# Splitting and multiplying four rows of the first output projection inside the Fourier stage

## The reference

```python
def fourier_mix(u):
    b, n, e = u.shape
    ug = u.reshape(b, n, N_FOURIER_GROUPS, FOURIER_GROUP_DIM).astype(jnp.float32)
    f = jnp.fft.fft2(ug, axes=(1, 3), norm='ortho').real
    return f.reshape(b, n, e).astype(u.dtype)

def gated_out(o, g, w_out):
    return (o * jax.nn.silu(g)) @ w_out

# in each layer, with gt from the conditioning vector
xp = xp + gt_p * op
xs = xs + gt_s * os_
```

## Time and profile before

| | |
|---|---|
| median of the runs | 2153.98 us |
| profiled execution | 2157.06 us |
| its span, first to last instruction | 2155.2 us |
| TensorE busy | 2096.4 us, 97% |
| VectorE busy | 1384.9 us, 64% |
| ScalarE busy | 923.2 us, 43% |
| mean granted TensorE clock | 0.989 |

### The profile page before, as it was taken

One profiled execution on the slowest core, in us unless ns is written; L12 is line 12 of the kernel. 1 busy time (PEld: TensorE's weight loads), 2 busy tenths in 40 slices (PEclk: granted clock), 3 DMA queues, 4 the chain that ended last, 5 costly groups with the idle time before them and its releaser, 6 DMA issues. The chain is left out here.

```text
span 2155.2 us, 33197 instructions
## 1 busy us (share of the span) xinstructions
PE 2096.4 (97%) x13347; PEld 2030.1 (94%) x13347; DVE 1384.9 (64%) x2062; ACT 923.2 (43%) x1738; POOL 1.6 (0%) x8
## 2 busy tenths in 40 slices
PE   6999999989999999999999999999999999999997
PEld 4999977989999999999999999989999999989997
DVE  7887864664258888888754422238888888875223
ACT  7321242242134333333433333337777777764220
POOL 0000000000000000000000000000000000000000
PEclk9999999999999999999999999999999999999998
DMA  8653442694234444555544544361444433307332
GB/s 334 200 181 134 137 154 96 251 321 154 65 119 169 154 145 146 157 160 145 171 162 174 212 159 157 137 231 69 167 167 167 167 147 137 123 1 269 106 129 88
DMA packets 125976, 342.70 MB, mean 159 GB/s; under 512 B 14465, under 2 KB 69889, under 8 KB 116609
## 3 DMA queue, kind: packets, MB, share of 16 engines
q1 hardware_dynamic: 125824, 340.61, 45.8%
HBM read 225.70 MB, written 114.82 MB: 158 GB/s over the span
## 5 line engine op out<-in xcount | busy, mean ns | idle before, releaser
L254 PE MATMUL o_ps<-o_y_hi,o_w 128*128 128x384 f32 x768 | 197.7, 337 | 9.9 <-DVE o_y_lo L2352 9.2
L2783 DVE TENSOR_REDUCE a_nmax<-a_ps 128x1 f32<-128x1152 f32 x127 | 171.8, 1353 | 51.0 <-PE a_ps L2591 51.0
L254 PE MATMUL a_ps<-o_y_hi,o_w 128*128 128x384 f32 x768 | 196.3, 335 | 1.2 <-DVE o_x_early L2360 0.7
L2625 PE MATMUL a_ps<-a_v_hi,a_at_hi 128*128 128x256 f32 x576 | 173.8, 302 | 0.0
L2692 ACT ACTIVATE a_e<-a_ps,a_nmax 128x1152 f32<-128x1152 f32 x127 | 155.4, 1224 | 34.2 <-DVE a_nmax L2783 34.2
L2625 PE MATMUL a_ps<-a_v_lo,a_at_hi 128*128 128x256 f32 x576 | 163.0, 283 | 0.0
L2625 PE MATMUL a_ps<-a_v_hi,a_at_lo 128*128 128x256 f32 x576 | 162.8, 283 | 0.0
L254 PEld LDWEIGHTS o_ps<-o_y_hi,o_w 128*128 128x128 f32 x768 | 140.3, 190 | 10.6 <-DVE o_y_lo L2352 9.3
L254 PEld LDWEIGHTS a_ps<-o_y_hi,o_w 128*128 128x128 f32 x768 | 138.8, 188 | 2.1 <-DVE o_x_early L2360 1.1
L2352 DVE TENSOR_TENSOR o_y_lo<-o_y_raw,o_y_hi 128x384 fp32r<-128x384 f32 x94 | 51.1, 556 | 133.1 <-ACT o_y_hi L2301 133.1
L2701 ACT CAST a_at_hi<-a_ps 128x512 fp32r<-128x512 f32 (+1 forms) x192 | 91.5, 476 | 91.0 <-PE a_ps L2606 91.0
(11 more groups left out here) (370 smaller groups left out, 5781.8 us busy)
## 6 DMA issues: line engine op xcount, KB each, us to landing
p_w_raw<-w_in_dram SPq DMA_DIRECT2D x32, 1024.0 KB, 4.9
o_y_raw<-y_dram SPq DMA_DIRECT2D x96, 192.0 KB, 3.6
g_wada<-w_ada_dram SPq DMA_DIRECT2D x32, 512.0 KB, 4.5
f_w_raw<-w_u_dram SPq DMA_DIRECT2D x32, 512.0 KB, 4.4
o_w_raw<-w_out_dram SPq DMA_DIRECT2D x28, 512.0 KB, 5.0
g_dram<-g_stage SPq DMA_DIRECT2D x16, 576.0 KB, 3.1
f_g<-g_dram SPq DMA_DIRECT2D x8, 1152.0 KB, 7.7
y_dram<-f_y SPq DMA_DIRECT2D x8, 1152.0 KB, 5.5
```

The source lines that it names most:

```text
L254: mm = pe.matmul(ps[:, d, 0:CH], a, m, start=(e == 0 and j == 0), stop=(e == ET - 1 and j == 2))
L2625: mm = pe.matmul(ps[:, out_bank(at_step), 0:UC], a, x, start=(kt == 0 and j == 0), stop=(kt == TT - 1 and j == 2))
L2783: dve.tensor_reduce(nmax[:, m % 2, half:half + 1], ps[:, 3 * half:3 * half + 3, 0:CH], AX.XY, ALU.max, negate=True).then_inc(maxed, 1)
```

## The change

Rows 0 to 3 of w_out and the y tiles 0 to 3 of chunk 0 get a raw tile of their own, `stage`, with 8 KB for each row. SP issues the four loads of w in iteration 2 of the Fourier stage ahead of the wait for `gated`, and the four loads of y between the store of y of unit 2 and the load of g of unit 5. Iteration 6 now loads the second set: w rows 4 to 7 and the y tiles that follow in the order.

ScalarE splits the staged operands behind unit 6's casts (w for output tiles 4 and 5, 512 columns each, and the four y tiles) and behind unit 7's (w for tiles 6, 7 and 3). VectorE makes their low halves ahead of `gate(5)`, `gate(6)` and `gate(7)`. TensorE multiplies rows 0 to 3 for the output tiles 4 to 7 behind spectra(7), within the Fourier block, into the banks 0 to 3, and tiles 3, 0, 1, 2 at the start of the projection's block; PSUM is kept over the boundary, and output tile d of layer 0 has another bank. Then the projection goes on at row 4. `gate(n)` starts at a new semaphore, `halves_done` (the end of L1882), and waits for `chan_done` before the context columns; the `spectrum_lo` between its parts move by one place each. The split y tiles of layer 0 lie in other places, ScalarE waits for the last y stores at row 10, and `ab_lo` has its own address. Layer 1 keeps its order.

```diff
+    STAGED = (4, 0)
+    BANKS = ((5, 6, 7, 4, 0, 1, 2, 3), range(DT))
+    STAGED_D, WAITING_D, LATER_D = (4, 5, 6, 7), 3, (0, 1, 2)
...
+    def staged_raw(self, d):
+
+        return self.stage[:, :, BANK + d * P:BANK + (d + 1) * P]
+
+    def staged_hi(self, act, d, done):
+        act.copy(self.w[:, d, 0, 0:self.staged, :], self.staged_raw(d)).then_inc(done, 1)
+
+    def staged_lo(self, dve, d, done):
+        dve.tensor_tensor(self.w[:, d, 1, 0:self.staged, :], self.staged_raw(d), self.w[:, d, 0, 0:self.staged, :].bitcast(F32),
+                          ALU.subtract).then_inc(done, 1)
...
+    def load_next(self, eng, y_src, w_src):
+        for p, (c, e) in enumerate(self.order[self.NR:2 * self.NR]):
+            self.load_y(eng, y_src, self.NR + p, c, e)
+            self.load_w(eng, w_src, self.staged + p)
...
                 if n == H - 2:
                     sp.wait_ge(tok_done, first_piece[H - 1] + 4)
-                    ahead(sp)
+                    following.load_next(sp, y_rows, w_out)
+                if n == 2:
+                    sp.wait_ge(tok_done, first_piece[3] + 4)
+                    for e in range(following.staged):
+                        following.load_w(sp, w_out, e)
                 sp.wait_ge(gated, n + 1)
                 sp.dma_start(y_d[n], y[:, s]).then_inc(y_out[s], 16)
+                if n == 2:
+                    sp.wait_ge(y_out[1], 16)
+                    for e in range(following.staged):
+                        following.load_y(sp, y_rows, e, 0, e)
                 if n + 3 < H:
                     sp.dma_start(g[:, n % 3], g_d[n + 3]).then_inc(g_in[n % 3], 16)
...
+                mm.then_inc(halves_done, 1)
                 if n >= 1:
                     pe.wait_ge(ctx_gated, n)
...
+            def staged_products(k, es):
+
+                pe.wait_ge(following.ahead_lo, k + 1)
+                for e in es:
+                    pe.wait_ge(following.y_lo_done, e + 1)
+                    following.products(pe, ps, following.STAGED_D[k], e)
+
+            for es in (range(0, 2), range(2, 4)):
+                for k in range(2):
+                    staged_products(k, es)
+            staged_products(2, range(4))
+            pe.wait_ge(gated, H - 1)
+            staged_products(3, range(4))
...
+                if n == H - 2:
+                    for e in range(following.staged):
+                        act.wait_ge(following.w_in[e], 16)
+                    for d in following.STAGED_D[0:2]:
+                        following.staged_hi(act, d, following.ahead_hi)
+                    for e in range(following.staged):
+                        following.first_y_hi(act, e)
+            act.wait_ge(tok_done, first_piece[H - 1] + 4)
+            for d in (*following.STAGED_D[2:4], following.WAITING_D):
+                following.staged_hi(act, d, following.ahead_hi)
...
-                dve.wait_ge(chan_done, n + 1)
+                dve.wait_ge(halves_done, n + 1)
...
-                if n + 2 < H:
-                    spectrum_lo(n + 2, 0)
+                dve.wait_ge(chan_done, n + 1)
...
                 if n + 2 < H:
-                    spectrum_lo(n + 2, 1)
+                    spectrum_lo(n + 2, 0)
...
             for n in range(H):
+                if n == H - 3:
+                    for k in range(2):
+                        staged_lo(k)
+                if n == H - 2:
+                    for e in range(2):
+                        following.first_y_lo(dve, e)
+                if n == H - 1:
+                    for e in range(2, 4):
+                        following.first_y_lo(dve, e)
+                    dve.wait_ge(chan_done, H)
+                    for k in range(2, 5):
+                        staged_lo(k)
                 gate(n)
...
+            if staged:
+                for k, d in enumerate((tiles.WAITING_D, *tiles.LATER_D)):
+                    if k == 0:
+                        pe.wait_ge(tiles.ahead_lo, len(tiles.STAGED_D) + 1)
+                    else:
+                        pe.wait_ge(tiles.later_lo, k)
+                    for e in range(staged):
+                        mm = products(d, e)
+                        if k == len(tiles.LATER_D):
+                            mm.then_inc(e_done, 1)
             for c in range(LAST):
-                for e in range(ET):
+                for e in range(staged if c == 0 else 0, ET):
...
+            if staged:
+                for d in tiles.LATER_D:
+                    tiles.staged_hi(act, d, tiles.later_hi)
+                act.wait_ge(tiles.later_lo, len(tiles.LATER_D))
             for e in range(ET):
+                if staged and e == 6 + staged:
+                    for semaphore, count in stored:
+                        act.wait_ge(semaphore, count)
```

More of the change, by code:

```diff
@@ L218, in tile @@
             return nc.alloc_sbuf_tensor_at(f"o{layer}_{name}", shape, F32, offset=sh.base + offset)
+        self.staged, self.banks = self.STAGED[layer], self.BANKS[layer]
+        if self.staged:
+            self.stage = tile("stage", [P, self.staged, 4 * BANK], 114688)
         self.y_raw = tile("y_raw", [P, self.NR, CH], 180224)
@@ L229, in __init__ @@
         self.x_out = [nc.alloc_semaphore(f"o{layer}_x_out{d}") for d in range(DT)]
+    LAG = 4
+    order = []
+    for e in range(ET):
+        order += [(0, e)] + ([(1, e - LAG)] if e >= LAG else [])
+    for e in range(ET - LAG, ET):
+        order += [(1, e)]
+    for e in range(ET):
+        order += [(2, e)]
     def begin(self, nc, sh, layer):
-        w_at, y_at = ((49152, 0), (0, 131072))[layer]
+        w_at = (49152, 0)[layer]
         def at(name, shape, offset):
@@ L252, in products @@
     def products(self, pe, ps, d, e):
-        for j, (a, m) in enumerate(passes(self.w[:, d, 0, e, :], self.w[:, d, 1, e, :], self.y_hi[:, e, :], self.y_lo[:, e, :])):
-            mm = pe.matmul(ps[:, d, 0:CH], a, m, start=(e == 0 and j == 0), stop=(e == ET - 1 and j == 2))
+        for j, (a, m) in enumerate(passes(self.w[:, d, 0, e, :], self.w[:, d, 1, e, :], self.y[0][e], self.y[1][e])):
+            mm = pe.matmul(ps[:, self.banks[d], 0:CH], a, m, start=(e == 0 and j == 0), stop=(e == ET - 1 and j == 2))
         return mm
     def w_hi(self, act, e, ds=slice(0, DT)):
[L258 to L261, removed]
+        act.wait_ge(*self.row_in(e))
         act.copy(self.w[:, ds, 0, e, :], self.raw(e, ds)).then_inc(self.w_hi_done, 1)
     def w_lo(self, dve, e, ds=slice(0, DT)):
-        dve.wait_ge(self.w_hi_done, e + 1)
+        dve.wait_ge(self.w_hi_done, e - self.staged + 1)
         dve.tensor_tensor(self.w[:, ds, 1, e, :], self.raw(e, ds), self.w[:, ds, 0, e, :].bitcast(F32),
@@ L1603, in _, with fourier_mix @@
                     own_attention(j, at)
[L1606 removed]
+def fourier_mix(nc, sh, fold, w_u, w_ny, g_d, y_d, dft_tok, dft_chan, following, y_rows, w_out):
     with ExitStack() as ctx:
@@ L2133, in out_project @@
         LAST = NCH - 1
-        if layer == 0:
-            tiles.begin(nc, sh, layer)
-        AHEAD = (0, 2)[layer]
-        if AHEAD > 0:
-            for semaphore in (tiles.ahead_hi, tiles.ahead_lo):
+        staged = tiles.staged
+        AHEAD = staged or 2
+        for semaphore in (tiles.ahead_hi, tiles.ahead_lo):
+            sh.own(semaphore)
+        if staged:
+            for semaphore in (tiles.later_hi, tiles.later_lo):
                 sh.own(semaphore)
-        w, y_hi, y_lo = tiles.w, tiles.y_hi, tiles.y_lo
         done_x = at("done_x", [P, LAST, DT, CH], 0)
-        w_raw, y_raw, x, sq, NR = tiles.w_raw, tiles.y_raw, tiles.x, tiles.sq, tiles.NR
-        if ps is None:
-            ps = ctx.enter_context(nc.psum_tensor(f"o{layer}_ps", [P, 8, BANK], F32))
+        x, sq, NR, banks = tiles.x, tiles.sq, tiles.NR, tiles.banks
+        LOADED = 2 * NR if staged else NR
         for semaphore, count in stored:
@@ L2166, in out_project @@
             y_stored = sem("y_stored")
-        LAG = 4
-        order = []
-        for e in range(ET):
-            order += [(0, e)] + ([(1, e - LAG)] if e >= LAG else [])
-        order += [(1, e) for e in range(ET - LAG, ET)] + [(2, e) for e in range(ET)]
-        place = {step: k for k, step in enumerate(order)}
+        LAG = tiles.LAG
+        place = {step: k for k, step in enumerate(tiles.order)}
         def chunk(c):
@@ L2195, in _ @@
             for e in range(ET):
-                if e >= tiles.NW:
-                    sp.wait_ge(w_lo_done, e - 3 if e < tiles.NW + 2 else e - 1)
+                p = e - staged
+                if p >= tiles.NW:
+                    sp.wait_ge(w_lo_done, p - 3 if p < tiles.NW + 2 else p - 1)
                     tiles.load_w(sp, w_src, e)
@@ L2373, in normalise @@
                 dve.scalar_tensor_tensor(tile, tile, sh.final_g[:, d:d + 1], factor, ALU.mult, ALU.mult).then_inc(normed, 1)
+            if staged:
+                for k, d in enumerate(tiles.LATER_D):
+                    dve.wait_ge(tiles.later_hi, k + 1)
```

(1 more changed line is left out.)

80 lines of the change are left out of this document (52 added, 28 removed).

## The result

The changed kernel takes 2143.0 us, median of six executions (2140.9 to 2147.4), against 2153.8 for the kernel before in the same session: ratio 0.995 [0.994, 0.996], 10.8 us less. Five executions on another chip gave 2145.2 against 2154.4, ratio 0.9957 [0.9943, 0.997], 9.2 less. The forecast was 8.6 less.

What follows compares the result with a forecast made beforehand. TensorE, busy 2096.4 of 2155.2 us, was taken as the bound, leaving its idle time and slow clock to win. 11.7 - 0.8 - 2.3 = 8.6 us less gave a median of 2145.4 us, range 2142.9 to 2150.5.

Steps and rivals of the forecast that it cites:

- The hole and its echo: Between Fourier stage and first out projection: TensorE idles 9.2 us, then slow clock costs 2.5; filling it wins 11.7 us.
- The operands: Late Fourier stage: ScalarE's added casts (3.3 us) and VectorE's low halves (5.7 us) fit; VectorE's end covered by 1.3 us.
- The boundary: Barrier ending the Fourier block: still costs TensorE 0.8 us, bounds 0.4 and 3.3, too short to slow the clock.
- The loads: Fourier units: 2.89 MB added to the shared queue delays small row loads, mainly unit 7's; TensorE loses 2.3 us.
- The 2 us behind the last byte: DMA fixed cost that would land unit 7's rows at 441.8 and make the loss 3.8 us; rejected from the trace.
- Behind the boundary: Start of the projection: y row 4 ready with 1.5 us of cover after the last y store, TensorE runs on as before.
- A: Rival: rows do not wait behind the added loads, or the queue has more room; loss 0 to 0.5, 2143.3 us; 15%.
- the prediction's own sign: Fourier units: TensorE waits of some 1 us ahead of unit 5's and unit 7's spectra if right; none would show otherwise.
- B: Rival: queue costs about 3 us more, through unit 7's rows, the last y store or staged y tiles; 2148.4 us; 25%.
- C: Rival: new VectorE order starves the token stage in every unit; 3.4 us slower, 2157.4 us; 4%.
- D: Rival: the hole only moves, within the staged products or after the barrier, with slow clock; gain under 3 us, 2152; 6%.

Runs made afterwards that it cites:

- Experiments 1: Changed kernel with all 48 staged products moved from the Fourier block to the start of the next block, loads and splits kept; 2154.6 us, ratio 1.0.
- 2: Changed kernel with 24 of the 48 staged products (tiles 6 and 7) moved to the start of the projection; 2149.2 us, ratio 0.9979.
- 3: Changed kernel with the gating's old order, waiting for all of a unit's spectra, low halves back where they stood; 2145.2 us, ratio 0.9963.
- 5: Kernel before with only the eight added loads (2.89 MB), into a free buffer read by nobody; 2157.2 us, ratio 1.001.
- 6: Changed kernel with the four staged w rows issued behind the store of y of unit 2, not ahead of it; 2145.6 us, ratio 0.9954.
- 7: Changed kernel with two staged w rows issued ahead of the store of y of unit 2 and two behind; 2144.8 us, ratio 0.9952.
- 9: Changed kernel with 1.05 MB of further unused loads in iteration 2 among the staged w rows; 2148.3 us, ratio 0.9969.
- 10: Changed kernel with 1.76 MB of further unused loads in iteration 2 among and behind the staged w rows; 2150.0 us, ratio 0.9978.
- experiment 4: Kernel before with only the new order of the gating and its low halves; 2153.3 us, ratio 0.9994.
- experiment 11: Kernel before with the load of g issued ahead of the store of y in every unit; 2156.2 us, ratio 1.0004.

## Why the prediction was right, and where its sum was off

**The hole and its echo, 11.7 us: right.** 135.92 - 125.02 = 10.9, with 0.3 at the boundary and 0.3 in the units given back, is 11.5. Experiments 1 and 2 show it by moving the products back.

**The operands: right.** ScalarE and VectorE in the changed kernel's unit 6, and VectorE's last low halves and last step of gating:

```profile
424.10 1.14 ACT L290 CAST o_w<-o_stage 128x512 fp32r<-128x512 f32 x2
...
425.14 1.76 ACT L326 CAST o_y<-o_stage 128x384 fp32r<-128x384 f32 x4
426.19 1.27 DVE L293 TENSOR_TENSOR o_w<-o_stage,o_w 128x512 fp32r<-128x512 f32 x2
...
440.42 1.88 DVE L293 TENSOR_TENSOR o_w<-o_stage,o_w 128x512 fp32r<-128x512 f32 x3
...
446.43 0.67 DVE L2195 TENSOR_TENSOR f_y<-gf_ps,f_g 1x512 f32<-1x512 f32 x1
```

The casts take 2.9 us (3.3 forecast), the low halves 5.2 in all (5.7). VectorE ends at 447.1 and TensorE at 448.4: 1.3 us of cover, as forecast.

**The boundary, 0.8: too dear.** It measured 0.3, less than the 0.4 of the lower bound. The 0.8 came from a boundary at which VectorE was last and ScalarE first; here TensorE is last and first.

**The loads, 2.3 us: the term that failed.** The step was "the queue is full while it moves, 357 GB/s, so 6.6 us a unit". Measured: TensorE lost 0.34 in the units. The changed kernel's queue while the added loads drain, and the microsecond after:

```profile
414.00:433.00 19.00, 18.88 (x159) 18.77 (x158) 16.42 (x48) 7.87 (x19) 0.00 (x0) 1.00 1.03 415
433.00:434.00 1.00, 1.00 (x11) 1.00 (x10) 1.00 (x3) 0.64 (x2) 0.00 (x0) 1.00 0.60 235
```

With work always waiting the queue moves 415 GB/s, not the 357 of the earlier trace rows, which is a mean over bursts that begin on an idle queue. By this rate, from the end of unit 1's transfers at 409.3: 7.08 MB of three units and the new 2.89 take 24.0 us, to 433.3, and it ran empty near 433.6. The last small packets, the rows of unit 7, pass by 434.0, and unit 7's spectra start at 435.58: about 1 us of slack, their landing counted, where the prediction had 2.3 of loss. At unit 5 there is almost none, and there the prediction was nearer: it had 0.9 of loss, and experiments 2, 3, 5, 6, 7 and 9 each show TensorE standing for the rows (0.15 to 1.84 us), until about 0.6 us after their last packet. The 2 us behind the last byte, which the prediction weighed from the Trainium skill (DMA: Bandwidth & Descriptors, section Anatomy of one DMA) and turned down, do not show for these rows; the page gives the figure for transfers that GpSimd issues, and here SP issues them. The row from which the rate could have been taken stood in the trace of before: 413 GB/s at a share of 1.03 behind the hole; its neighbour in the earlier trace rows, with a backlog too, has 384. The prediction took 384 for the new loads alone and the mean with its start for the rest.

**What it did not see: the stores.** A store of y issued behind the added loads lands in 10.5 us:

```profile
y_dram<-f_y SPq DMA_DIRECT2D x1, 1152.0 KB, 10.5
```

against 5.3 before, and VectorE may not write the next gated tile into that buffer until it has. VectorE, and the token product behind it:

```profile
420.01 1.22 DVE L2169 TENSOR_TENSOR f_y<-gf_ps,f_g 128x1024 f32<-128x1024 f32 x1 [2.40 <-DMA y_dram<-f_y]
```

```profile
422.79 0.19 PEld L1917 LDWEIGHTS gf_ps<-f_tok_hi,f_u_hi 128*128 128x128 f32 x1 [0.23 <-DVE f_ab_lo L2152]
```

2.40 us on VectorE come out as 0.2 to 0.3 on TensorE, which is all that the loads cost here. But neither this path nor that of the rows has cover left: experiment 9 turns one more megabyte into 4.1 us, on both. The prediction bounded the loads by the small rows alone and never named the path of the stores; its range held the time without having weighed it.

**Behind the boundary: right.** VectorE waits for the last y store and has y row 4 ready in time:

```profile
454.33 0.56 DVE L2465 TENSOR_TENSOR o_y<-o_y_raw,o_y 128x384 fp32r<-128x384 f32 x1 [0.80 <-DMA y_dram<-f_y]
```

It ends at 454.9; TensorE reaches row 4 at 448.67 + 8.3 = 457.0, 2.1 us later (1.5 forecast).

**The rivals.** A has the nearest time, 2143.3, in part for its reason (more room in the queue), and by the prediction's own sign, no waits ahead of the spectra of units 5 and 7, it is A that came; its other reason, that rows do not queue, is refuted by experiment 6. B was a real neighbour: experiments 9 and 10 are B, by the rows of unit 5 and a store of y where it named unit 7's rows and the last store. C is refuted by experiment 4, though the wait it describes, the fourth token piece for the low half of the first, is the one by which a late store reaches TensorE. D did not occur.

**The order of the gating: a gain of 1.1 us** (experiment 3) that the prediction used for VectorE's idle time and did not price by itself. It is why the boundary is 0.3 and not 0.7 and why less is lost in the units.

## What to carry to other kernels

Work that needs nothing from the stage's end belongs in front of the barrier, where TensorE would otherwise pause: it pays the pause and the slow clock behind it, here a fifth of the gain. Before loads are put in front of others in a queue, follow all that queues behind them, stores above all, to the engine that may not overwrite their source; and size the queue by its rate with a backlog, not by the mean over bursts. Ask how many microseconds are left before the queue, not the engine, decides: here none ahead of a store or of the small rows, and one more megabyte, 2.5 us of transfer, cost 4.1. And where a profile names a releaser, check in the code that the instruction waits for that one and when it ended: in experiment 9 it had not been waited for at all.

## What was not expected of the hardware

- One queue moved 415 GB/s over 19 us with a backlog and 357 over a burst from idle. Within such bursts some 2 us run at 217 to 295 GB/s, read from windows of 1 us. With store and load exchanged (experiment 11) the slow part stays; its cause is open.
- A pause of 3.70 us was followed by 3.4 us at granted clock 0.51, the 8.21 us of experiment 1 by some 5. In experiment 9 two pauses of 1.2 and 1.3 us with 1 us of work between were followed by 3.2 us at 0.50; behind the single wait of 1.84 in experiment 6 it stayed at 1.00.
- Where TensorE waited for the small row loads (2.3 KB), it started some 0.6 us after their last packet: their landing adds no more than that.
- Phases at 0.50 come and go. Behind the boundary after the projection the changed kernel had none in its first profile and some 6 us in its second; near 65 us, before anything that the kernels differ in, some kernels show one and others none. An effect of this size has to be read in the stretch it belongs to.
